# Experts of a decoder layer: down products one block behind, in three single-pass products, with low parts cut on POOL

## The chip, the cores and the metric

One core of a Trainium2 chip. The metric is the device time of one launch in microseconds; smaller is better. All arithmetic is on float32 data.

## The reference

One decoder layer over 1024 prompt tokens and 8 sample tokens, width 1024. A combined projection feeds twelve dilated and eight stick-breaking attention heads and two gates; the heads' outputs are merged and added to `x`. Then comes a mixture of experts, an input embedding and a last norm. The part that matters here:

```python
def expert_block(args):
    xi, ei = args
    return (jax.nn.silu(xi @ w_gate[ei]) * (xi @ w_up[ei])) @ w_down[ei]

def channel_and_ple(x, p, ...):
    x = x + hier_moe(rmsnorm(x, g_moe), ...)
    gate = jax.nn.sigmoid(rmsnorm(x, g_ple) @ w_pg)
    return x + gate * (p @ w_pp)
```

Each token goes to the top two experts of its group. There are 32 experts, with `w_gate` and `w_up` of 1024 x 512 and `w_down` of 512 x 1024. Tokens are sorted by expert and handled in blocks of 128 rows, each with the weights of one expert.

## The kernel before

The kernel is written engine by engine, with semaphores set by hand. Its stages follow each other: `norm_in`, `project`, `stick_and_gates`, `dilated`, `decode`, `merge`, `residual`, `route`, `experts`, `finish`. In the trace a tile of the experts has the prefix `x_`, one of the last stage `f_`, one of the residual stage `r_`.

`residual` (L1433) makes `h`, nine tiles of 128 rows (the last has 8), which stays in SBUF until `finish` adds the experts' rows to it. `route` (L1550) writes the normed rows to DRAM in expert order (`xs`), and a table with each block's expert and first row.

`experts` (L1742) runs 32 blocks here. For one block SP loads the rows `x` (512 KB), `wg` and `wu` each in two halves of 1024 KB, and `wd` (2048 KB). TensorE multiplies float32 in two ways. A plain product of 128x512 takes float32 operands as they are (down, L1854). The other way (`products`, L82) splits each operand in a high part, rounded to the type fp32r, and the rest, and adds three single-pass products:

```python
    pe.matmul(out, w_low, m_high, start=first, stop=False)
    pe.matmul(out, w_high, m_low, start=False, stop=False)
    return pe.matmul(out, w_high, m_high, start=False, stop=last)
```

ACT makes the high parts (`high`, L1885: `wgh`, `wuh`; `xh`, L1901), and DVE the low parts by a subtraction (`low`, L1932: `wgl`, `wul`; `xl`, L1926). Gate and up have 8 k-slices each, so 24 products each; down has 4 k-slices and two halves of the output, 8 plain products in the code, each of which stands as two records in the trace.

The order of work is fixed for each engine in a function `step`. PE runs gate and up of a block (`gate_up`), turns the next block's rows (`turn`, L1829), then turns the hidden rows `hm` of the first block (`tph`, L1847) and multiplies them (`down`). DVE's `hidden` (L1942) makes `hm`, its `hidden_T` (L1947) copies the turned rows to `hT`. ACT takes the sigmoid (L1878) and copies the output out of PSUM (`output`, L1891), and POOL stores it to `ys` (L1981) at a row that it loads from the table. `passes` does the first two steps outside the loop and two steps for each turn of it. `need(eng, sem, v)` is a wait that is left out where `v` is not positive.

`finish` (L1991) gathers each token's two rows from `ys`, adds them to `h` (L2173), loads and splits the weights of the last projections in five pieces of 1 MB, and waits on DVE for the last gains `gf` before the second tile is turned.

Of the kernel before, what the change touches and what calls it, by code (L numbers as in the profile page):

```python
# [1432 lines left out]
def residual(nc, g, x_of):  # L1433

    ctx = ExitStack()
    with ctx:
# [113 lines left out]
def route(nc, g):  # L1550
# [5 lines left out]
    with ctx:  # L1556
# [95 lines left out]
        def _(dve):  # L1652
# [85 lines left out]
            then(dve.tensor_scalar(metaf[:, 2:3], metaf[:, 2:3], -1.0, None, ALU.add))  # L1738
# [3 lines left out]
def experts(nc, g):  # L1742
# [6 lines left out]
    with ctx:  # L1749
# [5 lines left out]
        wd = sb("wd", [P, 2, KF, D])  # L1755
        gm = sb("gm", [P, KD])
# [4 lines left out]
        hT = sb("hT", [P, KF, P])  # L1761
# [17 lines left out]
        Wd = g["w_down"].rearrange("a e (k p) f -> (a e) p k f", p=P)
        block = ctx.enter_context(nc.Block())  # L1780

        def pairs(eng):

            return eng.value_load(meta_row[0:1, 2:3], min_val=(-(-ASG // P) + 1) // 2 - 1,
                                  max_val=(MAXBLK + 1) // 2 - 1) + 1

        def passes(eng, step, end):


            n = pairs(eng)  # L1790
            for j in range(2):
                step(0, j)
            with eng.Fori(1, n) as it:
                for j in range(2):
                    step(it, j)
            if end:
                end(n)

        @block.sync
        def _(sp):  # L1800
            with nc.allow_non_contiguous_dma(reason="1024 gains, once"):
                sp.dma_start(gm[:, :], g["g_moe"].rearrange("a (k p) -> p (a k)", p=P)).then_inc(gm_in, 16)

            def step(it, b):
# [11 lines left out]
                need(sp, y_full, it * 4 + (2 * b - 2))  # L1816
# [5 lines left out]
        def _(pe):  # L1822
            def turn(it, b):

                pe.wait_ge(x_in[b], it * 16 + 16)
                for c in range(2):
                    need(pe, xT_full, it * 4 + (2 * b + c - 1))
                    for k in range(4):
                        last = pe.transpose(tpx[c][:, k, :], x[:, b, (c * 4 + k) * P:(c * 4 + k + 1) * P], ident[:, :])  # L1829
                    last.then_inc(tpx_full, 1)  # L1830

            def gate_up(n):

                pe.wait_ge(xl_full, n + 1)
                need(pe, hm_full, n)
                for bank, wh, wl, cut, s in ((G, wgh, wgl, gl_full, g_full), (U_, wuh, wul, ul_full, u_full)):
                    pe.wait_ge(cut, n * 2 + 2)
                    for k in range(KD):
                        last = products(pe, bank[:, :], xh[:, k, :], xl[:, k, :], wh[:, k, :], wl[:, k, :],
                                        k == 0, k == KD - 1)  # L1840
                    last.then_inc(s, 1)

            def down(p_, b, n):
                pe.wait_ge(hm_full, n + 1)
                need(pe, hT_full, n)
# [505 lines left out]
```

## Time and profile before

| | |
|---|---|
| median of 3 runs | 2381.64 us (2381.1 to 2393.33) |
| the profiled execution | 2380.5 us |
| its span | 2378.9 us |
| PE busy | 2012.9 us, 85% |
| DVE busy | 1098.7 us, 46% |
| ACT busy | 850.9 us, 36% |
| POOL busy | 277.5 us, 12% |
| mean granted TensorE clock | 0.92 |

The span is from the first instruction to the last of the profiled execution, and 1.6 us of its time lie around it. Busy shares are means over stages with different limits. A matmul record is longer than the distance to the next one, since they are pipelined, so a cost of PE is read from start to start.

### The profile page before, as it was taken

The page shows a single profiled execution, that of the slowest core. Times are in us where ns is not written, and L with a number is a line of the kernel's source. Part 1 is how long each engine was busy: PE and PEld are TensorE (multiplying, and loading weights), DVE is VectorE, ACT ScalarE, POOL GpSimd, SP SyncE. Part 2 cuts the span into 40 slices and gives each one's busy share as a digit, 9 for nine tenths or more (in the row PEclk, how much of TensorE's full clock was granted, in tenths as well). Part 3 has the DMA queues.
Part 4 walks back from the last instruction along what each step waited for, and adds up shares of the span by engine and source line. Part 5 has one row for each costly group of instructions (what it writes and reads, how often), then busy time and mean ns, then how long its engine had stood idle before and what let it go on. Part 6 is the DMA issues. An engine that isn't in the chain of part 4 may idle for free. (4 is left out here: it accounts for less than half of the span.)

```text
span 2378.9 us, 27707 instructions
## 1 busy us (share of the span) xinstructions
PE 2012.9 (85%) x10172; PEld 1572.0 (66%) x10172; DVE 1098.7 (46%) x1363; ACT 850.9 (36%) x1171; POOL 277.5 (12%) x356
## 2 busy tenths in 40 slices
PE   6999999698989879993288994499999999998598
PEld 5999999687878857772177452366666666665485
DVE  5212121255546545552342214466666666664564
ACT  4111111255546415450031100344444444452354
POOL 0110111143334310001012002100000000000210
PEclk8999999899999959896588996699999999999699
DMA  3343443434111042206334102999999999994530
GB/s 116 113 136 106 124 123 108 144 107 145 37 63 37 28 89 41 41 1 162 102 106 163 53 19 73 341 374 360 348 347 350 352 353 357 351 349 156 194 99 37
DMA packets 222238, 392.70 MB, mean 165 GB/s; under 512 B 29468, under 2 KB 100620, under 8 KB 222165
## 3 DMA queue, kind: packets, MB, share of 16 engines
q1 hardware_dynamic: 202916, 325.28, 40.3%
q0 software_dynamic: 14928, 50.60, 6.7%
q10 hardware_dynamic: 4320, 15.85, 1.7%
q8 instruction: 46, 0.75, 0.1%
q14 instruction: 28, 0.22, 0.0%
HBM read 321.02 MB, written 78.35 MB: 168 GB/s over the span
## 5 line engine op out<-in xcount | busy, mean ns | idle before, releaser
L1854 PE MATMUL x_Y<-x_wd,x_hT 128*128 128x512 f32 x512 | 229.8, 602 | 34.4 <-DVE x_hT L1947 34.4
L86 PE MATMUL p_acc<-uh,p_wl 128*128 128x344 f32 x720 | 234.9, 326 | 13.2 <-DVE ul L292 9.1
L88 PE MATMUL p_acc<-uh,p_wh 128*128 128x344 f32 x720 | 230.6, 320 | 0.0
L87 PE MATMUL p_acc<-ul,p_wh 128*128 128x344 f32 x720 | 230.4, 320 | 0.0
L1854 PEld LDWEIGHTS x_Y<-x_wd,x_hT 128*128 128x128 f32 x512 | 95.2, 191 | 150.1 <-issue 150.1
L304 DVE COPY p_zk<-p_tp 128x512 f32<-128x512 f32 (+1 forms) x90 | 44.2, 547 | 304.5 <-PE p_tp L225 304.5
L1932 DVE TENSOR_TENSOR x_wgl<-x_wg,x_wgh 128x2048 fp32r<-128x2048 f32 x64 | 146.3, 2286 | 69.9 <-ACT x_wgh L1885 69.9
L268 ACT ACTIVATE p_zc<-p_acc 128x344 f32<-128x344 f32 x90 | 41.2, 458 | 321.8 <-PE p_acc L88 321.8
L561 PE MATMUL g_acc<-uh,g_wl 128*128 128x344 f32 x384 | 131.2, 342 | 21.6 <-ACT u L594 19.5
L86 PEld LDWEIGHTS p_acc<-uh,p_wl 128*128 128x128 f32 x720 | 135.8, 189 | 18.1 <-issue 14.8
L1932 DVE TENSOR_TENSOR x_wul<-x_wu,x_wuh 128x2048 fp32r<-128x2048 f32 x64 | 143.5, 2282 | 0.0
L1485 PE MATMUL r_acc<-r_w,mT 128*128 128x512 f32 (+1 forms) x288 | 128.5, 606 | 10.0 <-DMA r_w<-in_w_out 10.0
L1885 ACT ACTIVATE x_wgh<-x_wg 128x2048 fp32r<-128x2048 f32 x64 | 118.9, 1906 | 49.1 <-DMA x_wg<-in_w_gate 49.1
L88 PEld LDWEIGHTS p_acc<-uh,p_wh 128*128 128x128 f32 x720 | 135.9, 189 | 0.0
L87 PEld LDWEIGHTS p_acc<-ul,p_wh 128*128 128x128 f32 x720 | 135.9, 189 | 0.0
L561 PE MATMUL g_acc<-ul,g_wh 128*128 128x344 f32 x384 | 129.7, 338 | 0.0
L561 PE MATMUL g_acc<-uh,g_wh 128*128 128x344 f32 x384 | 129.5, 337 | 0.0
L86 PE MATMUL x_G<-x_wgh,x_xl 128*128 128x512 f32 x256 | 114.8, 448 | 9.9 <-DVE x_xl L1926 9.9
L1885 ACT ACTIVATE x_wuh<-x_wu 128x2048 fp32r<-128x2048 f32 x64 | 118.4, 1896 | 0.1
L655 POOL TENSOR_TENSOR s_z<-s_z,s_w 128x1024 f32<-128x1024 f32 (+7 forms) x64 | 91.8, 1434 | 208.9 <-DVE s_w L682 208.9
L682 DVE TENSOR_TENSOR_SCAN s_w<-s_w,s_r 128x1024 f32<-128x1024 f32 (+7 forms) x64 | 86.8, 1356 | 54.9 <-ACT s_w L631 54.4
L820 PE MATMUL d_S<-d_k,d_q 64*128 64x256 f32 (+3 forms) x272 | 94.8, 499 | 17.4 <-DMA d_v<-ztok 16.9
(320 smaller groups left out, 4089.2 us busy)
## 6 DMA issues: line engine op xcount, KB each, us to landing
x_wg<-in_w_gate SPq DMA_DIRECT2D x64, 1024.0 KB, 7.3
x_wu<-in_w_up SPq DMA_DIRECT2D x64, 1024.0 KB, 7.3
x_wd<-in_w_down SPq DMA_DIRECT2D x32, 2048.0 KB, 12.1
x_x<-xs SPq DMA_DIRECT2D x32, 512.0 KB, 9.8
ys<-x_y POOLq DMA_DIRECT2D x32, 512.0 KB, 5.5
zT<-p_zc ACTq DMA_DIRECT2D x30, 516.0 KB, 3.4
p_w<-in_w_in SPq DMA_DIRECT2D x30, 512.0 KB, 5.5
ztok<-p_zk POOLq DMA_DIRECT2D x30, 512.0 KB, 4.6
```

Of the source, the lines that this page charges most:

```text
L86: pe.matmul(out, w_low, m_high, start=first, stop=False)
L87: pe.matmul(out, w_high, m_low, start=False, stop=False)
L88: return pe.matmul(out, w_high, m_high, start=False, stop=last)
L304: dve.tensor_copy(zk[0:r, b, t0:t0 + m, :], tp[j % 2][0:r, 0:m, :]).then_inc(zk_full, 1)
L561: last = pe.matmul(acc[grp % 2][:, 0:NS], lhs[:, c % 2, kk, :], rhs[:, kk, t], start=(x == 0), stop=(x == M - 1), skip_group_check=True)
L655: pool.tensor_tensor(z[:, u % ZB, 0:n], z[:, u % ZB, 0:n], w[:, u % WB, 0:n], ALU.subtract).then_inc(al_full, 1)
L682: dve.tensor_tensor_scan(w[:, u % WB, 0:n][:, ::-1], w[:, u % WB, 0:n][:, ::-1], r[:, u % 2, 0:n][:, ::-1], 0.0, ALU.add, ALU.add).then_in ...
L820: last = pe.matmul(S[x // 2][:, c:c + n], q[:, b, x, i * P:(i + 1) * P], k[:, b, x, key:key + n], start=True, stop=True, skip_group_check= ...
L1485: last = pe.matmul(acc[t % 2][0:r, c * 512:(c + 1) * 512], mT[:, k, t * P:t * P + r], w[:, k, c * 512:(c + 1) * 512], start=(k == 0), stop ...
L1854: last = pe.matmul(Y[c][:, :], hT[:, k, :], wd[:, b, k, c * 512:(c + 1) * 512], start=(k == 0), stop=(k == KF - 1))
L1885: act.activation(wh[:, HALVES[half], :], w[:, HALVES[half], :], ACT.Copy).then_inc(full, 1)
L1932: dve.tensor_tensor(wl[:, s, :], w[:, s, :], wh[:, s, :], ALU.subtract).then_inc(full, 1)
```

## The change

The down products are made in the same three-product way. For this `wd` is split too: ACT makes `wdh`, one k-slice at a time, and POOL makes `wdl` by a subtraction; the hidden rows are split to `hh` on ACT and `hl` on DVE. PE's step now has gate of block n, turning the hidden rows of block n-1, up of block n, turning the rows of block n+1, and down of block n-1. ACT copies the output of yet a block earlier at the start of its step, and issues the store to `ys` itself, with the row that it loads. DVE makes both halves of `wgl` ahead of `hm` and `xT`. Both halves of `wg` and `wu` are waited for one by one on PE.

The weights of the experts are read with rows p*k+j to partition p instead of j*128+p, so a partition reads four or eight rows that lie together, and PE turns columns with a stride to match.

To make room in SBUF, `h` isn't kept there over the experts: `residual` stores its nine tiles to `h_kept` in DRAM and `finish` loads them again, two ahead of the weight pieces and seven behind them, before `gf`. Four steps instead of two stand outside the loop.

```diff
+                if t >= 2:
+                    sp.dma_start(g["h_kept"][(t - 2) * P:(t - 1) * P, :], h[:, t - 2, :]).then_inc(h_out, 16)
+            for t in range(TT - 2, TT):
+                sp.wait_ge(h_full, t + 1)
+                sp.dma_start(g["h_kept"][t * P:t * P + rows(t), :], h[0:rows(t), t, :]).then_inc(h_out, 16)
+            sp.wait_ge(h_out, 16 * TT)
...
+        Wg = g["w_gate"].rearrange("a e (p k) f -> (a e) p k f", p=P)
+        Wu = g["w_up"].rearrange("a e (p k) f -> (a e) p k f", p=P)
+        Wd = g["w_down"].rearrange("a e (p k) f -> (a e) p k f", p=P)
...
+            n = eng.value_load(meta_row[0:1, 2:3], min_val=0, max_val=(MAXBLK + 1) // 2 - MINPAIR) + MINPAIR
+            for it in range(PEEL):
+                for j in range(2):
+                    step(it, j)
+            with eng.Fori(PEEL, n) as it:
                 for j in range(2):
                     step(it, j)
...
-                need(sp, y_full, it * 4 + (2 * b - 2))
+                need(sp, dl_full, it * 8 + (4 * b - 4))
                 sp.dma_start(wd[:, b, :, :], w(Wd)).then_inc(d_in[b], 16)
...
+                by_k = x[:, b, :].rearrange("t (p k) -> t k p", k=KD)
...
+            def gate(n):
                 pe.wait_ge(xl_full, n + 1)
+                need(pe, gs_full, n)
+                gate_or_up(n, G, wgh, wgl, gl_full, g_full)
...
+            def turn_hidden(n):
                 pe.wait_ge(hm_full, n + 1)
-                need(pe, hT_full, n)
+                need(pe, hl_full, n)
+                by_k = hm[:, :].rearrange("t (p k) -> t k p", k=KF)
                 for k in range(KF):
-                    last = pe.transpose(tph[:, k, :], hm[:, k * P:(k + 1) * P], ident[:, :])
+                    last = pe.transpose(tph[:, k, :], by_k[:, k, :], ident[:, :])
                 last.then_inc(tph_full, 1)
...
+            def down(n):
+                pe.wait_ge(hl_full, n + 1)
+                need(pe, y_read, n * 2)
+                for k in range(KF):
+                    pe.wait_ge(dl_full, n * 4 + (k + 1))
+                    for c in range(2):
+                        cols = slice(c * 512, (c + 1) * 512)
+                        last = products(pe, Y[c][:, :], hh[:, k, :], hl[:, k, :], wdh[:, k, cols], wdl[:, k, cols],
+                                        k == 0, k == KF - 1)
+                    last.then_inc(d_used, 1)
...
+                one, two = lag(it, j, 1), lag(it, j, 2)
+                if one:
+                    gate(one[0])
+                if two:
+                    turn_hidden(two[0])
+                if one:
+                    up(one[0])
+                turn(it * 2 + j, j, it)
+                if two:
+                    down(two[0])
...
+            def high_down(n, b, it):
+                act.wait_ge(d_in[b], it * 16 + 16)
+                for k in range(KF):
+                    need(act, d_used, it * 8 + (4 * b + k - 3))
+                    act.activation(wdh[:, k, :], wd[:, b, k, :], ACT.Copy).then_inc(dh_full, 1)
+
+            def high_hidden(n):
+                act.wait_ge(tph_full, n + 1)
+                need(act, d_used, n * 4)
+                act.activation(hh[:, :, :], tph[:, :, :], ACT.Copy).then_inc(hh_full, 1)
...
+            def output(n, b, it):
+                act.wait_ge(d_used, n * 4 + 4)
                 for c in range(2):
-                    act.wait_ge(y_full, n * 2 + c + 1)
                     act.activation(y[:, b, c * 512:(c + 1) * 512], Y[c][:, :], ACT.Copy).then_inc(y_read, 1)
+                need(act, y_out[1 - b], it * 16 + 16 * b)
+                act.wait_ge(y_read, n * 2 + 2)
+                row = act.value_load(meta_row[0:1, bass.ds(n * 4 + 1, 1)], min_val=0, max_val=ASG)
+                act.dma_start(ys[bass.ds(row, P), :], y[:, b, :]).then_inc(y_out[b], 16)
...
+                if three:
+                    output(*three)
+                if two:
+                    high_down(*two)
+                if one:
+                    sigmoid(one[0])
+                if two:
+                    high_hidden(two[0])
                 high(new, wg, wgh, wg_in, g_full, gh_full)
                 act.wait_ge(xT_full, new * 2 + 2)
+                need(act, u_full, new)
                 act.activation(xh[:, :, :], xT[:, :, :], ACT.Copy).then_inc(xh_full, 1)
                 high(new, wu, wuh, wu_in, u_full, uh_full)
...
+            def low_hidden(n):
+                dve.wait_ge(hh_full, n + 1)
+                dve.tensor_tensor(hl[:, :, :], tph[:, :, :], hh[:, :, :], ALU.subtract).then_inc(hl_full, 1)
...
+                if one:
+                    gated(one[0])
+                if two:
+                    low_hidden(two[0])
+                for half in range(2):
+                    low(new, half, wg, wgh, wgl, gh_full, gl_full)
+                if one:
+                    hidden(one[0])
                 turn(new)
-                low(new, 1, wg, wgh, wgl, gh_full, gl_full)
                 low_x(new)
                 for half in range(2):
                     low(new, half, wu, wuh, wul, uh_full, ul_full)
...
+            def low_down(n, b):
+                for k in range(KF):
+                    pool.wait_ge(dh_full, n * 4 + (k + 1))
+                    pool.tensor_tensor(wdl[:, k, :], wd[:, b, k, :], wdh[:, k, :], ALU.subtract).then_inc(dl_full, 1)
+
+            def step(it, j):
+                two = lag(it, j, 2)
+                if two:
+                    low_down(two[0], two[1])
...
+            def load_h(t):
+                sp.dma_start(h[0:rows(t), t, :], g["h_kept"][t * P:t * P + rows(t), :]).then_inc(hs_in[t], 16)
+
             for t in range(2):
                 sp.dma_start(pt[0:rows(t), t % 2, :], p_of(t)).then_inc(p_in[t % 2], 16)
+                load_h(t)
             for n, (raw, w, _, _) in enumerate(pieces):
                 need(sp, wl_full, n - 2)
                 sp.dma_start(raw, w).then_inc(piece_in[n], 16)
+            for t in range(2, TT):
+                load_h(t)
...
+                dve.wait_ge(hs_in[t], 16)
...
-            g["h"] = ctx.enter_context(nc.sbuf_tensor("h", [P, TT, D], F32, side="right"))
```

ACT, the second step in the loop of `experts`. Before:

```order
L1878 ACTIVATE x_sg<-x_G 128x512
L1884 ISA
L1885 ACTIVATE x_wgh<-x_wg 128x2048 x2
L1900 ISA
L1901 ACTIVATE x_xh<-x_xT 128x1024
L1885 ACTIVATE x_wuh<-x_wu 128x2048 x2
L1888 ISA
L1890 REGISTER_ALU
L1891 ACTIVATE x_y<-x_Y 128x512 x2
```

The same step of the changed kernel, from the output's copies on:

```order
L1934 ACTIVATE x_y<-x_Y 128x512 x2
L1936 ISA
L1937 ISA
L1937 TENSOR_LOAD meta_row
L1937 ISA x2
L1938 ISA
L1938 DMA ys<-x_y 128x1024
L60 REGISTER_ALU
L1924 ACTIVATE x_wdh<-x_wd 128x1024
```

Three more `x_wdh` follow, then `x_sg`, the new `x_hh`, and `x_wgh`, `x_xh` and `x_wuh` as before. The output's copies moved from the end of the step to its beginning, with the table's load and the store's issue behind them.

DVE, the same step. Before:

```order
L1936 TENSOR_TENSOR x_gs<-x_sg,x_G 128x512
L1930 ISA
L1932 TENSOR_TENSOR x_wgl<-x_wg,x_wgh 128x2048
L1942 TENSOR_TENSOR x_hm<-x_gs,x_U 128x512
L1947 COPY x_hT<-x_tph 128x512
L1920 TENSOR_TENSOR x_xT<-x_tpx,x_gm 128x512
L1919 REGISTER_ALU
L1920 TENSOR_TENSOR x_xT<-x_tpx,x_gm 128x512
L1932 TENSOR_TENSOR x_wgl<-x_wg,x_wgh 128x2048
```

And of the changed kernel:

```order
L1995 TENSOR_TENSOR x_gs<-x_sg,x_G 128x512
L2005 TENSOR_TENSOR x_hl<-x_tph,x_hh 128x512
L1988 ISA
L1990 TENSOR_TENSOR x_wgl<-x_wg,x_wgh 128x2048
L1988 REGISTER_ALU
L1990 TENSOR_TENSOR x_wgl<-x_wg,x_wgh 128x2048
L2001 TENSOR_TENSOR x_hm<-x_gs,x_U 128x512
L1978 TENSOR_TENSOR x_xT<-x_tpx,x_gm 128x512 x2
```

The second `x_wgl` moved ahead of `x_hm` and both `x_xT`; `x_xl` and two `x_wul` follow in both.

## Rows read from the trace of the kernel before

**Rows 1.** Page, 40 slices of 59.5 us: busy tenths of PE and of DMA.

```profile
PE   6999999698989879993288994499999999998598
...
DMA  3343443434111042206334102999999999994530
```

**Rows 2.** Stretches: bounds, length, busy us per engine, clock, DMA share, GB/s.

```profile
1600.00:1700.00 100.00, 94.91 (x358) 63.54 (x359) 63.84 (x49) 48.44 (x40) 2.66 (x5) 1.00 0.94 347
...
1805.00:1810.00 5.00, 3.83 (x21) 2.79 (x21) 3.15 (x5) 0.57 (x1) 0.00 (x0) 1.00 1.02 414
```

**Rows 3.** Waits, 1700 to 1909 us: total us, times, longest.

```profile
PE x_Y L1854 <- DVE x_hT L1947: 10.7, 10, 1.2
```

**Rows 4.** Tile x_G: ns min/median/max, first and last start.

```profile
L1878 ACT ACTIVATE x_sg<-x_G x32: 597/597/598, 1529.9 to 2177.2; 128x512 f32<-128x512 f32 x32
```

**Rows 5.** Timeline of one block: start, us, engine, line, operation, names.

```profile
1801.09 0.40 PE L86 MATMUL x_U<-x_wuh,x_xl 128*128 128x512 f32 x1
...
1806.45 0.40 PE L88 MATMUL x_U<-x_wuh,x_xh 128*128 128x512 f32 x1
...
1806.69 1.04 PE L1829 MATMUL x_tpx<-ident,x_x 128*128 128x128 f32 x8
...
1807.72 0.66 PE L1847 MATMUL x_tph<-ident,x_hm 128*128 128x128 f32 x4
...
1809.55 7.13 PE L1854 MATMUL x_Y<-x_wd,x_hT 128*128 128x512 f32 x16 [1.17 <-DVE x_hT L1947]
...
1816.11 0.80 PE L86 MATMUL x_G<-x_wgh,x_xl 128*128 128x512 f32 x1
```

**Rows 6.** Groups, 1700 to 1909 us: count | busy us, mean ns | idle.

```profile
L1932 DVE TENSOR_TENSOR x_wgl<-x_wg,x_wgh 128x2048 fp32r<-128x2048 f32 x21 | 48.0, 2287 | 12.2 <-ACT x_wgh L1885 12.2
...
L1885 ACT ACTIVATE x_wuh<-x_wu 128x2048 fp32r<-128x2048 f32 x20 | 36.9, 1895 | 0.0
...
L1920 DVE TENSOR_TENSOR x_xT<-x_tpx,x_gm 128x512 f32<-128x512 f32 x20 | 12.8, 680 | 0.0
...
L1901 ACT ACTIVATE x_xh<-x_xT 128x1024 fp32r<-128x1024 f32 x10 | 10.6, 1058 | 48.6 <-DVE x_xT L1920 48.6
...
L1942 DVE TENSOR_TENSOR x_hm<-x_gs,x_U 128x512 f32<-128x512 f32 x10 | 6.9, 686 | 8.8 <-PE x_U L88 8.8
```

**Rows 7.** Source line 1784, the counter's load: ns min/median/max, starts.

```profile
L1784 ACTq TENSOR_LOAD <-meta_row x1: 475/475/475, 1503.7 to 1503.7; - x1
...
L1784 ACTq FUSED_REGOPS  x1: 175/175/175, 1504.2 to 1504.2; - x1
```

**Rows 8.** Source line 1807, an address loaded on SP's queue.

```profile
L1807 SPq TENSOR_LOAD <-meta_row x32: 273/1424/1822, 1504.9 to 2132.4; - x32
```

**Rows 9.** Timeline of ACT at 301 us: a DMA issued from its queue.

```profile
301.10 0.34 ACTq L274 DMA_DIRECT2D zT<-p_zc  x1
```

**Rows 10.** POOL's groups over the whole span, columns as before.

```profile
L655 POOL TENSOR_TENSOR s_z<-s_z,s_w 128x1024 f32<-128x1024 f32 x8 | 19.0, 2376 | 38.2 <-DVE s_w L682 38.2
```

**Rows 11.** Source line 662, a 128x1024 difference on DVE.

```profile
L662 DVE TENSOR_TENSOR g_wl<-g_w,g_wh x16: 1211/1276/3052, 453.8 to 798.7; 128x1024 fp32r<-128x1024 f32 x16
```

**Rows 12.** Timeline, 557 to 560 us: POOL and DVE together.

```profile
557.69 2.37 POOL L655 TENSOR_TENSOR s_z<-s_z,s_w 128x1024 f32<-128x1024 f32 x1 [4.17 <-DVE s_w L682]
...
558.11 3.03 DVE L662 TENSOR_TENSOR g_wl<-g_w,g_wh 128x1024 fp32r<-128x1024 f32 x1
...
560.02 1.43 POOL L650 TENSOR_TENSOR s_z<-s_z,s_causal 128x128 f32<-128x128 f32 x1
```

**Rows 13.** Chain of waits, last stage: start, us, what.

```profile
2236.17 0.43 PE f_gate L88
```

**Rows 14.** DMA issues: names, queue, count, KB each, median us to landing.

```profile
f_gf<-in_g_final SPq DMA_DIRECT2D x1, 512.0 KB, 9.0
```

**Rows 15.** Timeline of the last stage.

```profile
2230.84 0.47 SPq L2050 DMA_DIRECT2D f_gf<-in_g_final  x1
...
2242.70 1.22 DVE L2194 TENSOR_TENSOR f_uT<-f_tp,f_gp 128x1024 f32<-128x1024 f32 x1
```

More of the change, by code:

```diff
@@ L1780, in experts @@
         block = ctx.enter_context(nc.Block())
-        def pairs(eng):
-            return eng.value_load(meta_row[0:1, 2:3], min_val=(-(-ASG // P) + 1) // 2 - 1,
-                                  max_val=(MAXBLK + 1) // 2 - 1) + 1
+        PEEL = 2
         def passes(eng, step, end):
[L1790 to L1793, printed above, removed]
+            n = eng.value_load(meta_row[0:1, 2:3], min_val=0, max_val=(MAXBLK + 1) // 2 - MINPAIR) + MINPAIR
[3 more added lines that the diff above has]
+            with eng.Fori(PEEL, n) as it:
@@ L1797, in passes, with lag @@
                 end(n)
+        def lag(it, j, back):
+            new = it * 2 + j
+            if isinstance(it, int) and new < back:
+                return None
+            return new - back, (j - back) % 2, it + (j - back) // 2
         @block.sync
@@ L1835, in gate_up, with up @@
+            def up(n):
                 need(pe, hm_full, n)
[L1836 to L1843, printed above, removed]
+                gate_or_up(n, U_, wuh, wul, ul_full, u_full)
@@ L1850, in down @@
-                pe.wait_ge(hT_full, n + 1)
-                for c in range(2):
-                    need(pe, y_read, n * 2 - 1 + c)
-                    for k in range(KF):
-                        last = pe.matmul(Y[c][:, :], hT[:, k, :], wd[:, b, k, c * 512:(c + 1) * 512],
-                                         start=(k == 0), stop=(k == KF - 1))
-                    last.then_inc(y_full, 1)
-            def step(it, j):
-                behind = j or not isinstance(it, int)
-                p_, b, n = (it, 0, it * 2) if j else (it - 1, 1, it * 2 - 1)
-                if behind:
-                    gate_up(n)
-                turn(it, j)
-                if behind:
-                    down(p_, b, n)
@@ new lines, in step @@
+            def step(it, j):
+                one, two = lag(it, j, 1), lag(it, j, 2)
[8 more added lines that the diff above has]
+                    down(two[0])
+            def end(np_):
+                last = np_ * 2 - 1
+                gate(last)
+                turn_hidden(last - 1)
+                up(last)
+                down(last - 1)
+                turn_hidden(last)
+                down(last)
@@ L1893, in step @@
             def step(it, j):
-                behind = j or not isinstance(it, int)
-                p_, b, n = (it, 0, it * 2) if j else (it - 1, 1, it * 2 - 1)
+                one, two, three = lag(it, j, 1), lag(it, j, 2), lag(it, j, 3)
                 new = it * 2 + j
-                if behind:
-                    sigmoid(n)
+                if three:
[4 more added lines that the diff above has]
+                    sigmoid(one[0])
@@ L1910, in _ @@
+                output(last - 2, 1, np_ - 2)
+                high_down(last - 1, 0, np_ - 1)
+                sigmoid(last)
+                high_hidden(last - 1)
+                output(last - 1, 0, np_ - 1)
+                high_down(last, 1, np_ - 1)
+                high_hidden(last)
+                output(last, 1, np_ - 1)
             passes(act, step, end)
@@ L2000, in finish @@
         C = D // 2
+        h = sb("h", [P, TT, D])
+        hs_in = [sem(f"h_in{t}") for t in range(TT)]
         wpgh, wpgl = (sb(n, [P, KD, D], F32R) for n in ("wpgh", "wpgl"))
```

95 lines of the change are left out of this document (40 added, 55 removed).

## The prediction

> **What bounds the kernel now.** I read the page's slices first: from about 1506 to 2196 us one stage, the experts, holds PE and the DMA engines at nine tenths or more together [rows 1]. It is the only long stage that the change rewrites. The reader is to see that shares do not tell which of the two ends last, so the waits come next: in ten blocks PE waits 10.7 us for x_hT, 1.07 each, and neither PE nor ACT or DVE waits for a transfer [rows 3]. The DMA engines move 347 GB/s over a hundred us and 414 in a stretch where they have work queued [rows 2], so they have room. One block moves 7.34 MB (four halves of 1024 KB, x_wd of 2048, x_x and ys of 512 each): at 400 GB/s 18.4 us.
>
> The length of a block is read from the sigmoid x_sg: 32 of them start between 1529.9 and 2177.2 us [rows 4], so 647.3 / 31 = 20.9 us. The timeline of one block fills that with PE alone [rows 5]: the 24 products of up begin from 1801.09 to 1806.45, 0.233 apart (5.36 / 23), gate costs as much, so 48 x 0.233 = 11.2; transposes 1.04 and 0.66; the wait for x_hT 1.17; the down products, eight of two records each, 6.56 (1809.55 to 1816.11), 0.82 a product; the first gate product 0.80 for 0.40, which delays those behind it by some 0.3. Sum 20.9. **PE sets the block.**
>
> **PE after the change.** Eight products at 0.82 become 24 single-pass ones, whose spacing stands above: 5.6 for 6.56. The wait of 1.17 goes, since x_hm is a step old when PE turns it and up stands between its halves and their use. PE needs 72 x 0.233 + 1.7 = 18.5 us, 2.4 less. The transposes now read with a stride; no row shows that. Between nothing and double (1.7 more) PE is still under the loop below, so I price it at nothing: what hides it is PE's own slack of 5 us, without which it costs up to 1.7 a block.
>
> **ACT and DVE after the change.** What is late next is a loop that exists now but has slack. In one step ACT does, in order: x_y twice, an address load with its DMA, x_wdh four times, x_sg, x_hh, x_wgh twice, x_xh, x_wuh twice. DVE does x_gs, x_hl, x_wgl twice, x_hm, x_xT twice, x_xl, x_wul twice. x_xh waits for x_xT, which stands on DVE behind both x_wgl; the next step's x_y stands on ACT behind x_wuh. The terms:
>
> - x_y: 2 x 0.6 = 1.2, by x_sg, which is of its shape [rows 4].
> - Load and issue, new on ACT's queue and behind a wait for its own x_y: load 0.48, register work 0.18 [rows 7], issue 0.34 [rows 9], together 1.0. The load's upper bound is 1.42, SP's median just behind its DMA issues [rows 8]; ACT's issue is a step old, so I take 0.48. Queued behind it are all of ACT's copies. The removed POOL issue gave PE nothing: POOL waited for ACT.
> - x_wdh: same shape as x_xh, 1.06 each, so 4.2; x_sg and x_hh 0.6 each [rows 4].
> - x_wgh, x_wuh 1.9 each [rows 6], x_wgl 2.29, x_hm 0.69, x_xT 0.68, x_xh 1.06.
>
> With nothing in the way: 1.2 + 1.0 + 4.2 + 1.2 + 1.9 (the first x_wgh), then DVE 4.6 + 0.7 + 1.4, then ACT 1.1 + 3.8 = 21.1; back-to-back instructions overlap by up to 0.1, hand-overs cost up to 0.1, and I take 20.7. PE's gain of 2.4 is already gone here: this loop is within 0.2 of the old block.
>
> **The shared port.** The new x_wdl is 128x1024 with two inputs in SBUF on POOL. Its nearest row is L655's form of the same shape, 2.38 us [rows 10], 9.5 for four. Does that run beside DVE's x_wgl, which also reads two SBUF tiles? The trace has such pairs. g_wl on DVE takes 1.21 at the least and up to 3.05 [rows 11]. At 558.11 it started 0.42 after POOL's s_z, which held on to 560.06: 1.95 of waiting, and 3.03 - 1.95 = 1.08 of work. POOL's next s_z of 128x128, begun at 560.02, took 1.43 instead of under half a microsecond: it waited for DVE in turn [rows 12]. The engines alternate; they do not share. By the Trainium skill's page "SBUF — State Buffer", section "Who interferes with whom", the second read interface is an exclusive lock held for a whole instruction; the trace agrees.
>
> So in a block, POOL's four x_wdl start when the first x_wdh is done, 1.2 + 1.0 + 1.1 = 3.3 us into ACT's step, and alone would end at 12.8. DVE asks for x_wgl at 9.5. It waits for the third x_wdl, runs one x_wgl, waits for the fourth, runs the other: 3.3 us lost. The loop reads 3.3 + 9.5 (POOL) + 4.6 (both x_wgl) + 0.7 + 1.4 + 1.1 + 3.8 = 24.4, less the same 0.4: **24.0 us a block**, 3.1 more than now. x_wul and x_xl fall outside that stretch. The DMA engines (7.34 MB in 24.0) and PE (18.5) both get slack.
>
> The Trainium skill's page "GPSIMD Engine Reference", section 3.1, measures a two-input operation on GpSimd at about 2.6 cycles an element. At the 1.2 GHz it gives, that is an estimate of 2.2 us for 1024; by it the block would be 23.4 and the kernel 19 us less. The row of 2.38 is this kernel's own, and the sum goes by it.
>
> **Two ends.** Steps 0 and 1 have none of ACT's and POOL's new work, 2 x 3.1 saved; the last block's x_wdl (9.5) has nothing over it. About +4, bounds -6 and +12.
>
> **h through DRAM.** Nine stores of 512 KB in the residual stage go on SP's queue, each behind a load; that stage leaves the DMA engines nearly idle [rows 1] and its last store is one tile of 8 rows: nothing, bounded by one landing of some 3 us. In the last stage two h loads go ahead of the weights and seven, 3.2 MB, ahead of f_gf. f_gf took 9.0 us to land [rows 14]; at 400 GB/s the loads put 8 us on it. DVE waits for it before f_uT at 2242.70, where f_gf, issued at 2230.84, had been there for 3 us [rows 15]. So +5, and 2 for the first two loads: +7, bounds 0 and 13. The larger runs of the expert weights (four and eight rows together) are at nothing: nobody waits for them, before or after.
>
> **Sum**, against the profiled execution's own 2380.5 us (the median of the three runs is 1.1 above it): 31 x 3.1 = 96, + 4, + 7 = +107: **2488 us**. Above and below 0.5%, 12 us, a measurement can tell it from no change.
>
> **Rivals.**
> 1. DVE goes first whenever the port comes free. Then it waits once, 1.0, and not twice: block 21.7, 31 x 0.8 + 11 = +36, 2417. For: a single kind of hand-over is on record. Against: POOL's s_z at 560.02 had come second and ran next.
> 2. POOL and DVE don't disturb each other in this stage, or the four x_wdl are over before DVE asks: block 20.7 or 20.5, 31 x -0.4 + 11: 2380, no change. Against it stand [rows 11, 12] and x_wdl's 9.5 us against the 6.2 between first x_wdh and x_wgl; it decides where x_wdl takes under 1.6 us.
> 3. Not slower at all: the loop has a slack that I don't see (ACT's copies run ahead), and PE's 18.5 holds: 31 x -2.4 + 11 = -63, 2317. It needs x_xh to come 2.2 us sooner. Against: every copy's order is fixed.
> 4. PE falls to its lower clock. Idle for 5 us in each block, it could come back at 1.2 GHz, where the last stage's products of this shape stand 0.43 apart [rows 13]. If gate and up both run so: 48 x 0.43 + 24 x 0.233 + 1.7 = 27.9, 31 x 7.0 + 11 = +228, 2609. If gate alone does, PE ends its block inside the 24.0 and it costs nothing. The Trainium skill's page "TensorE: Matmul & The Clock Gate", rules for authors, warns of such gaps between bursts. I find it less likely for both, because PE would then be busy all the time.
>
> The upper bound of the load adds 0.9 a block (28 us); an x_wdl slower by a tenth (its output type has no row on POOL) 29: 2545 together.
>
> **How the numbers follow.** The forecast 0.70, rival 1 0.12, rival 2 0.07, rival 3 0.05, rival 4 0.06. The range holds the forecast with its bounds and rival 1, 2400 to 2545, and leaves the other three out, 0.18. Faster 0.05, no change 0.07, slower 0.88.
>
> **What would show it.** Right: x_sg 24 us apart; x_wgl well over its 2.29 in the mean, near 4; some x_wdl over 4 us; PE's longest wait for x_xl, not for x_hl; the DMA share down to eight tenths; POOL at 300 us more or above; f_uT's second start later by 5. Wrong: x_wgl at 2.29 (rival 2), x_wdl long and x_wgl short (1), gate and up at 0.43 (4), ACT idle before x_y. If x_sg stands 24 apart with x_wgl undisturbed, the load on ACT was the cost and my reason fails.

## The result, and the profile after

| | before | after |
|---|---|---|
| median of four runs each, us | 2385.8 (2381.1 to 2393.33) | 2481.29 (2479.04 to 2487.31) |
| ratio | | 1.040, 95% interval 1.036 to 1.044 |
| profiled execution, us | 2380.5 | 2481.67 |
| block of the experts, mean of 31 (us) | 20.9 | 23.4 |

The changed kernel is slower by 4.0%. The forecast was 2488, in the range 2400 to 2545; the profiled execution came out 6 us under it.

The two kernels were timed beside each other. Beside the experiments below the kernel before has medians of 2389.3, 2393.0 and 2389.4 us, and all ratios are to it.

The slices of the page first, as in [rows 1] but of 62.0 us each, and one window of the experts with the columns of [rows 2]:

```profile
PE   5999999698898699953689953888888888887498
...
DMA  3434433541210403034343119787777877873720
```

```profile
1700.00:1940.00 240.00, 202.97 (x864) 162.29 (x863) 172.84 (x102) 142.37 (x131) 119.73 (x42) 0.93 0.77 308
```

In the experts (the long run of eights in PE) DMA is at seven and eight tenths where [rows 1] have nines, and PE at eight: the transfers wait for something else, and so does PE. The granted clock is 0.93 of full, for 1.00 before. The sigmoid, as in [rows 4] (nanoseconds min/median/max, first and last start):

```profile
L1911 ACT ACTIVATE x_sg<-x_G x32: 572/577/599, 1536.3 to 2262.6; 128x512 f32<-128x512 f32 x32
```

(2262.6 - 1536.3) / 31 = 23.43 us a block, for 20.88. 31 x 2.55 = 79 of the 101 us that the profiled executions lie apart. The mean of 31 hides one thing: the first two distances are 19.55 and 22.60, since the first two steps lack part of the new work, and the other 29 have a mean of 23.59. Where blocks are compared below it is by the mean of 31; where the forecast of one block is judged, by 23.59.

Now one block, in the timeline (start, length, what; in brackets the idle time before and what ended it), from one x_xh to the next:

```profile
1803.57 1.06 ACT L1954 ACTIVATE x_xh<-x_xT 128x1024 fp32r<-128x1024 f32 x1 [7.67 <-DVE x_xT L1978]
1804.53 3.70 ACT L1918 ACTIVATE x_wuh<-x_wu 128x2048 fp32r<-128x2048 f32 x2
...
1808.13 1.06 ACT L1934 ACTIVATE x_y<-x_Y 128x512 f32<-128x512 f32 x2
...
1809.97 0.34 ACTq L1938 DMA_DIRECT2D ys<-x_y  x1
...
1810.44 3.90 ACT L1924 ACTIVATE x_wdh<-x_wd 128x1024 fp32r<-128x1024 f32 x4 [1.24 <-issue]
...
1811.57 11.57 POOL L2037 TENSOR_TENSOR x_wdl<-x_wd,x_wdh 128x1024 fp32r<-128x1024 f32 x4 [11.98 <-ACT x_wdh L1924]
...
1814.86 0.69 DVE L1995 TENSOR_TENSOR x_gs<-x_sg,x_G 128x512 f32<-128x512 f32 x1 [3.90 <-ACT x_sg L1911]
...
1817.14 8.15 DVE L1990 TENSOR_TENSOR x_wgl<-x_wg,x_wgh 128x2048 fp32r<-128x2048 f32 x2 [1.00 <-ACT x_wgh L1918]
...
1825.22 0.68 DVE L2001 TENSOR_TENSOR x_hm<-x_gs,x_U 128x512 f32<-128x512 f32 x1
...
1825.82 1.28 DVE L1978 TENSOR_TENSOR x_xT<-x_tpx,x_gm 128x512 f32<-128x512 f32 x2
...
1827.13 1.06 ACT L1954 ACTIVATE x_xh<-x_xT 128x1024 fp32r<-128x1024 f32 x1 [8.21 <-DVE x_xT L1978]
```

This is the loop, 23.56 us round, and each step of it is read off from start to start: x_xh 0.96, both x_wuh 3.60, both x_y with the load and the issue 2.31, the first x_wdh 1.13, then 5.57 to the start of x_wgl and 8.08 to its end, x_hm 0.60, x_xT and the hand-over 1.31. The two rows of 11.57 (POOL's x_wdl) and 8.15 (DVE's x_wgl) are the ones to look at. Two such subtractions take 4.49 where POOL is idle (the x_wul below), and here 8.15. Where each one waited is told by their tiles (rows of x_wgl and x_wul on DVE, of x_wdl on POOL):

```profile
L1990 DVE TENSOR_TENSOR x_wgl<-x_wg,x_wgh x64: 2286/3744/4494, 1519.9 to 2245.3; 128x2048 fp32r<-128x2048 f32 x64
```
```profile
L1990 DVE TENSOR_TENSOR x_wul<-x_wu,x_wuh x64: 2283/2289/2294, 1529.2 to 2256.7; 128x2048 fp32r<-128x2048 f32 x64
```
```profile
L2037 POOL TENSOR_TENSOR x_wdl<-x_wd,x_wdh x128: 2352/2415/4485, 1550.8 to 2284.6; 128x1024 fp32r<-128x1024 f32 x128
```

x_wul is the same operation on the same shape, in a stretch where POOL is idle, and never takes over 2.3. x_wgl, beside POOL's x_wdl, takes 3.74 in the median and up to 4.49; one x_wdl of a block takes 4.49 too, for 2.4: about its own time behind one x_wgl's. The row of x_gs in the timeline shows what is not shared: it lies inside the stretch of x_wdl and keeps its 0.69 (so do all 32 of them), with one input in SBUF and the other (x_G) in PSUM.

The waits between 1700 and 1940 us, ten blocks (total us, times, longest):

```profile
PE x_G L87 <- DVE x_xl L1984: 36.7, 10, 4.8
ACT x_wdh L1924 <- issue: 12.8, 10, 1.3
```

PE waits for x_xl, 4.8 at the longest, never for x_hl, and once, for 0.2, for x_wdl. ACT waits 1.27 a block in which the profile names nobody: its own row load and DMA issue. In the last stage the gains f_gf now take 13.7 us to land, and DVE waits 4.99 for them (views as in [rows 14, 15]):

```profile
f_gf<-in_g_final SPq DMA_DIRECT2D x1, 512.0 KB, 13.7
```

```profile
2341.65 1.23 DVE L2266 TENSOR_TENSOR f_uT<-f_tp,f_gp 128x1024 f32<-128x1024 f32 x1 [4.99 <-DMA f_gf<-in_g_final]
```

### The profile page after: what moved, and what is told of

The parts are those of the page before. It is cut to its first block and busy times, and to the rows that moved or that the text cites. A ratio compares the mean times of both kernels' runs of the same rounds, so it can differ in the third digit from the quotient of the medians.

```text
span 2480.0 us, 28841 instructions
## 1 busy us (share of the span) xinstructions
PE 2020.7 (81%) x10428; PEld 1656.9 (67%) x10428; DVE 1206.8 (49%) x1363; ACT 984.8 (40%) x1332; POOL 627.8 (25%) x451
## 5 line engine op out<-in xcount | busy, mean ns | idle before, releaser
L2037 POOL TENSOR_TENSOR x_wdl<-x_wd,x_wdh 128x1024 fp32r<-128x1024 f32 x128 | 367.0, 2903 | 415.8 <-ACT x_wdh L1924 415.8
L1990 DVE TENSOR_TENSOR x_wgl<-x_wg,x_wgh 128x2048 fp32r<-128x2048 f32 x64 | 250.9, 3958 | 64.3 <-ACT x_wgh L1918 64.3
L87 PE MATMUL p_acc<-uh,p_wl 128*128 128x344 f32 x720 | 234.5, 326 | 14.1 <-DVE ul L293 9.8
L87 PE MATMUL x_G<-x_wgh,x_xl 128*128 128x512 f32 x256 | 124.2, 485 | 126.4 <-DVE x_xl L1984 126.4
L87 PEld LDWEIGHTS x_G<-x_wgh,x_xl 128*128 128x128 f32 x256 | 59.6, 233 | 153.9 <-issue 121.2
L1924 ACT ACTIVATE x_wdh<-x_wd 128x1024 fp32r<-128x1024 f32 x128 | 124.9, 1047 | 39.9 <-issue 39.9
L1954 ACT ACTIVATE x_xh<-x_xT 128x1024 fp32r<-128x1024 f32 x32 | 33.8, 1056 | 251.9 <-DVE x_xT L1978 251.9
L316 POOL DMA_DIRECT2D ztok<-p_zk x30 | 28.0, 933 | 394.4 <-DVE p_zk L305 380.1
```

What stands on the lines that cost most here:

```text
L1924: act.activation(wdh[:, k, :], wd[:, b, k, :], ACT.Copy).then_inc(dh_full, 1)
L1990: dve.tensor_tensor(wl[:, s, :], w[:, s, :], wh[:, s, :], ALU.subtract).then_inc(full, 1)
L2037: pool.tensor_tensor(wdl[:, k, :], wd[:, b, k, :], wdh[:, k, :], ALU.subtract).then_inc(dl_full, 1)
```

## The experiments

In this section GpSimd is the engine that the traces call POOL, VectorE is DVE, ScalarE ACT, TensorE PE and SyncE SP. Theory: POOL's x_wdl and DVE's x_wgl exclude each other at their reads of SBUF, and this lies in the loop above, with ACT's load and issue as a second term. Rivals: that ACT's and POOL's mere lengths close the loop; that the move, without any split, is what costs; that the larger runs of the layout matter. Twelve runs follow, one of them the changed kernel once more. All have the changed kernel's order and h in DRAM where nothing else is said.

**GpSimd only writes.** x_wdl becomes two memsets with two tiny subtractions (a wait between the two pairs is not shown):

```
-pool.tensor_tensor(wdl[:, k, :], wd[:, b, k, :], wdh[:, k, :], ALU.subtract)
+pool.tensor_tensor(wdl[:, k, 0:4], wd[:, b, k, 0:4], wdh[:, k, 0:4], ALU.subtract)
+pool.memset(wdl[:, k, 8:D].bitcast(F32), 0.0)       # then the same on 4:8 and 8:D
```

> The changed kernel, but GpSimd only writes: instead of each subtraction of x_wdl it does two memsets of 128x1016 and two subtractions of 128x4, about 2.2 to 2.5 us a slice, so nearly as long as the subtraction (2.38). The low part of the down weights is left out. Theory (the two subtractions, GpSimd's and VectorE's, wait for each other at their reads of SBUF): x_wgl goes from a mean of 3.96 us back to 2.29, x_wdl's place takes no longer than its own time, and the block goes from 23.4 to about 20.7 us, the kernel from 2481 to about 2400. Rival (the loop is closed by ScalarE's row load and DMA issue and by GpSimd's mere length): x_wgl may fall, but the block stays at 23.0 to 23.4 and the kernel at 2470 to 2481.

Measured: 2378.93 us in one run, block 20.26.

```profile
L1912 ACT ACTIVATE x_sg<-x_G x32: 570/574/602, 1536.5 to 2164.5; 128x512 f32<-128x512 f32 x32
```

```profile
1823.59 0.20 POOL L2041 TENSOR_TENSOR x_wdl<-x_wd,x_wdh 128x4 fp32r<-128x4 f32 x1
...
1824.63 1.35 POOL L2038 TENSOR_TENSOR x_wdl<-x_wd,x_wdh 128x4 fp32r<-128x4 f32 x1
...
1825.92 0.94 POOL L2039 MEMSET x_wdl<- 128x1016 f32 x1
...
1826.10 2.29 DVE L1991 TENSOR_TENSOR x_wgl<-x_wg,x_wgh 128x2048 fp32r<-128x2048 f32 x1 [0.17 <-ACT x_wgh L1919]
...
1826.95 1.50 POOL L2041 TENSOR_TENSOR x_wdl<-x_wd,x_wdh 128x4 fp32r<-128x4 f32 x1
```

The timeline is the experiment in small. The memset at 1825.92 keeps its 0.94 beside x_wgl, and x_wgl keeps 2.3 beside memsets (2.33 at the most in all 64). The subtraction of 128x4 at 1824.63, of 0.20 elsewhere, takes 1.35, until x_wgl ends at 1825.92; the one at 1826.95 takes 1.50, until the second x_wgl ends at 1828.39. GpSimd's queue is as long as before (2.2 us a slice for 2.4), so its length isn't what cost: the reads are. 3.2 us a block come back, and the block is 0.4 shorter than the 20.7 expected.

**GpSimd copies, one input.** In two forms: one copy a slice, then, since the first said nothing, two.

```
-pool.tensor_tensor(wdl[:, k, :], wd[:, b, k, :], wdh[:, k, :], ALU.subtract)
+pool.tensor_copy(wdl[:, k, 8:D], wdh[:, k, 8:D])    # once, behind a subtraction of 128x8; or twice, each behind one of 128x4
```

> The changed kernel, with a copy of x_wdh (one input) on GpSimd in place of each two-input subtraction of x_wdl, behind a subtraction of 128x8 (the low part of the down weights is left out). With GpSimd writing only, VectorE kept its x_wgl at 2.29 us. Theory (what is shared is the second read): with one input GpSimd does not hold it; x_wgl 2.3 us, block 20.2, kernel about 2380. Rival (any read by GpSimd holds it): x_wgl at 3 to 3.5, since the copy is shorter (1.1 to 1.3 us), block 21 to 22, kernel 2400 to 2430.

Measured: 2371.09 us in one run, block 19.95; x_wgl 2.29. But the timeline shows that the last copy was over before x_wgl began, so neither side was put to the test:

```profile
1817.49 1.03 POOL L2038 CAST x_wdl<-x_wdh 128x1016 fp32r<-128x1016 f32 x1
...
1819.49 4.49 DVE L1990 TENSOR_TENSOR x_wgl<-x_wg,x_wgh 128x2048 fp32r<-128x2048 f32 x2 [1.00 <-ACT x_wgh L1918]
```

> As the run in which GpSimd only wrote, with each memset replaced by a copy (one input) of x_wdh, about 1.03 us each, so that a slice takes 2.3 to 2.4 us and the copies stand beside VectorE's x_wgl (the low part of the down weights is left out). Theory (only an instruction with two inputs takes the second read): copies keep 1.03 us and x_wgl 2.29 beside each other; the tiny two-input subtractions of 128x4 wait for x_wgl to end; block about 20.2, kernel about 2378. Rival (any read of GpSimd excludes VectorE): x_wgl above 3 us or copies above 2 us, block 21.5 or more, kernel above 2400.

Measured: 2433.66 us in one run, block 21.64.

```profile
L1912 ACT ACTIVATE x_sg<-x_G x32: 572/577/599, 1546.1 to 2217.0; 128x512 f32<-128x512 f32 x32
```

```profile
1807.39 4.73 DVE L1991 TENSOR_TENSOR x_wgl<-x_wg,x_wgh 128x2048 fp32r<-128x2048 f32 x2 [1.00 <-ACT x_wgh L1919]
...
1807.86 2.12 POOL L2041 TENSOR_TENSOR x_wdl<-x_wd,x_wdh 128x4 fp32r<-128x4 f32 x1
...
1809.92 3.09 POOL L2042 CAST x_wdl<-x_wdh 128x1016 fp32r<-128x1016 f32 x1
```

My theory of the "second read" falls and the rival holds: the copy at 1809.92, one input, takes 3.09 for 1.03, since it stands until the second x_wgl is done. VectorE waits too: x_wgl takes 2.58 in the mean of the window and up to 3.13, for 2.31 and 2.33 beside memsets. So GpSimd's one-input copy and VectorE's two-input subtraction exclude each other too; a memset and VectorE don't. Not all of the time is lost at the port. The block is 1.4 us longer than with memsets, and only about 0.5 of it lies in the two x_wgl. About 0.9 lies in ACT's waits for the transfer of x_wg, 16.9 us in eleven blocks for 7.9 in twelve: SP issues x_wd's load only when GpSimd's last copy is done, and x_wg's stands behind it in the queue. The Trainium skill's page "SBUF — State Buffer", section "Who interferes with whom", has it so: VectorE's instruction with two SBUF inputs contends with a GpSimd instruction that reads SBUF, not with one that only writes. Both of these runs agree, with 3.09 and 0.94 us. For the kernel it changes nothing, since its x_wdl has two inputs.

**x_wdl on VectorE.**

```
-pool: low_down(two[0], two[1])
+dve:  low_down(two[0], two[1])      # ahead of gated(one[0]); in the end ahead of gated and of the last low_hidden
```

> The changed kernel, with the subtractions of x_wdl on VectorE (4 of 128x1024, about 1.2 us each, ahead of x_gs) and none on GpSimd. Theory (shared reads): x_wgl at 2.29, no instruction above its own time; VectorE has 4.9 us more work but gets back 3.4 of x_wgl and had idle time before x_gs and x_hl; block 20.7, kernel about 2400 (2385 to 2425). Rival (the work itself is too much for the loop, wherever it stands): block 23 to 24.5, kernel 2470 to 2515.

Measured: 2383.93 us (2373.79 to 2394.58, ten runs), 0.995 of the kernel before (0.992 to 0.998); block 20.05, for 20.7 expected. The second row is the window 1700 to 1940 us, its columns those of [rows 2].

```profile
L1911 ACT ACTIVATE x_sg<-x_G x32: 571/576/600, 1555.6 to 2177.2; 128x512 f32<-128x512 f32 x32
```

```profile
1700.00:1940.00 240.00, 220.17 (x1003) 177.10 (x1002) 212.17 (x169) 168.50 (x156) 0.00 (x0) 1.00 0.96 366
```

The same arithmetic, and 3.4 us a block are back: 4.9 us of added work on the busier engine cost about 0.1 (20.05, beside 19.95 in the run with one copy a slice), where 9.6 us on the idle one cost 3.4 (23.43 - 20.05). The window's clock is 1.00 again.

**Store of ys from GpSimd.**

```
-act: row = act.value_load(...); act.dma_start(ys[...], y[:, b, :])
+pool: row = pool.value_load(...); pool.wait_ge(y_read, ...); pool.dma_start(ys[...], y[:, b, :])   # ahead of low_down
```

> The changed kernel, with the row load and the issue of the store of ys moved from ScalarE back to GpSimd, ahead of its x_wdl. Theory (ScalarE's 1.27 us between x_y and x_wdh are a term of the loop): x_wdh starts 1.27 earlier in each block and the block goes to about 22.2, the kernel to about 2443 (2435 to 2455). Rival (only the shared port and GpSimd set the block, and GpSimd now takes the load itself): no change, 2475 to 2485.

Measured: 2459.79 us (2455.69 to 2476.84), 1.030 (1.023 to 1.037); block 22.65, 0.78 less and not 1.2, and the kernel above the range expected.

```profile
L1912 ACT ACTIVATE x_sg<-x_G x32: 584/598/599, 1534.4 to 2236.6; 128x512 f32<-128x512 f32 x32
```

```profile
1799.23 3.90 ACT L1925 ACTIVATE x_wdh<-x_wd 128x1024 fp32r<-128x1024 f32 x4
...
1800.57 11.95 POOL L2041 TENSOR_TENSOR x_wdl<-x_wd,x_wdh 128x1024 fp32r<-128x1024 f32 x4
...
1805.93 8.74 DVE L1988 TENSOR_TENSOR x_wgl<-x_wg,x_wgh 128x2048 fp32r<-128x2048 f32 x2 [1.00 <-ACT x_wgh L1919]
```

ACT's 1.27 us are gone, but from the start of x_wdh to the end of the second x_wgl it is now 15.44 us, for 14.85 in the block of the changed kernel shown above. The pair of x_wgl itself is not a steady sign: it takes 6.7 to 8.7 from block to block, as x_wgl starts sooner or later, and the stretch takes 15.4 in those blocks too. The 0.59 lie on POOL, whose x_wdl let x_wgl through last: it begins 0.21 later against x_wdh, and its first x_wdl, right behind the issue of the store, takes 2.79 for 2.41. 1.27 - 0.59 = 0.68 of the measured 0.78. So half of ACT's gain was lost because the load and the issue now stand ahead of x_wdl on POOL, which is the rival in part.

**The move alone.** x_hh in f32, eight products as before, no x_wdh, x_wdl, x_hl:

```
-last = products(pe, Y[c][:, :], hh[:, k, :], hl[:, k, :], wdh[:, k, cols], wdl[:, k, cols], ...)
+last = pe.matmul(Y[c][:, :], hh[:, k, :], wd[:, b, k, cols], ...)
-need(sp, dl_full, it * 8 + (4 * b - 4))
+need(sp, d_used, it * 8 + (4 * b - 4))
```

> The move alone: the down products stand behind the next block's gate and up as in the changed kernel, h goes through DRAM, but the down weights and the hidden values stay f32 and whole, 8 products instead of 24, no x_wdh, x_wdl, x_hl. Theory (TensorE bound the kernel of before, and 1 to 1.5 us of it a block was a wait for the turned hidden values that the move covers): block 19.5, kernel about 2360 (2345 to 2385). Rival (the wait only moves elsewhere, to the low parts of x): block 20.9, kernel 2395 to 2410, above the kernel before by the h loads.

Measured: 2462.57 us (2461.55 to 2472.09), 1.030 (1.024 to 1.036); block 22.76. Neither theory nor rival. SyncE's queue (SPq) and ACT's wait:

```profile
L1910 ACT ACTIVATE x_sg<-x_G x32: 597/598/599, 1540.5 to 2246.2; 128x512 f32<-128x512 f32 x32
```

```profile
1710.55 0.33 SPq L1831 DMA_DIRECT2D x_wd<-in_w_down  x1
1712.39 0.33 SPq L1825 DMA_DIRECT2D x_x<-xs  x1
1712.98 0.91 SPq L1829 DMA_DIRECT2D x_wg<-in_w_gate  x2
```

```profile
ACT x_wgh L1917 <- DMA x_wg<-in_w_gate: 34.1, 10, 6.4
```

x_wd's buffer is used by products that now stand two steps behind, so its load waits until 1710.55, and x_x, x_wg and x_wu of the next block stand behind it in the queue. ACT then waits for x_wg's transfer, up to 6.4 us. The mean of 22.76 is made of two kinds of block: they alternate between 19.3 and 25.7 to 27.5 us, and why only every other one pays is not shown. The next run moves that one load:

```
 for dst, src, cut, done in ((wg, ...), (wu, ...)): ...
-need(sp, d_used, it * 8 + (4 * b - 4)); sp.dma_start(wd[:, b, :, :], w(Wd))
+if one: load_down(*one)             # the x_wd of the block before, its own row of the table
```

> The move alone (f32 down products behind the next block's gate and up), but the load of a block's x_wd is issued one step later, behind the next block's x_wg and x_wu. In the run before, SyncE's queue waited at x_wd for the down products two blocks back, until 1710.55, and the x_x, x_wg and x_wu behind it landed late (ScalarE's x_wgh waited for their transfers 34.1 us in ten blocks). Theory (the place of that wait in the queue made the move alone slow, not the products): block 19.5 to 20.2, kernel 2360 to 2385. Rival (TensorE's f32 down products between up and the next gate hold back x_xT and the low parts whatever the loads do): block stays at 22 to 22.8, kernel 2440 to 2465.

Measured: 2355.83 us (2351.44 to 2368.01), 0.986 (0.981 to 0.990); block 19.43.

```profile
L1920 ACT ACTIVATE x_sg<-x_G x32: 597/598/600, 1535.1 to 2137.3; 128x512 f32<-128x512 f32 x32
```

```profile
1705.10 2.53 SPq L1829 DMA_DIRECT2D x_wu<-in_w_up  x2
1709.45 0.33 SPq L1837 DMA_DIRECT2D x_wd<-in_w_down  x1
1711.29 0.33 SPq L1825 DMA_DIRECT2D x_x<-xs  x1
```

```profile
1700.00:1940.00 240.00, 240.00 (x935) 165.24 (x934) 157.78 (x111) 129.83 (x113) 0.00 (x0) 1.00 0.96 377
```

3.3 us a block from the place of one load. PE is busy for the whole 240 us of the window, and the block is what the prediction's terms give for it: 11.2 + 1.7 + 6.56 = 19.5. So the move by itself is a gain of 1.5 us a block, the wait of [rows 3] and some start-up, once nothing queues behind it.

**The old layout,** on the version with x_wdl on VectorE:

```
-"a e (p k) f -> (a e) p k f"
+"a e (k p) f -> (a e) p k f"        # and so for g_moe, x and hm
```

> The kernel with x_wdl on VectorE, with the old layout of the expert weights, x and h (row k*128+p on partition p, as before the change). With the new layout this stage moves 366 GB/s at a DMA share of 0.96 between 1700 and 1940 us, 381 per full share; the kernel before moves 352 at 0.95, 370. Theory (that kernel is now bound by the DMA engines and the new layout is worth 3% of their rate): block 20.6 against 20.05, kernel 15 to 20 us slower than it. Rival (the share is high but something else ends last; forecast: the layout costs and gains nothing): the same within 5 us.

Measured: 2375.53 us (2371.91 to 2383.03), 0.993 (0.990 to 0.996); block 20.04.

```profile
L1911 ACT ACTIVATE x_sg<-x_G x32: 572/577/601, 1537.4 to 2158.5; 128x512 f32<-128x512 f32 x32
```

```profile
1700.00:1940.00 240.00, 225.61 (x1006) 179.94 (x1005) 212.17 (x168) 168.54 (x156) 0.00 (x0) 0.97 1.01 366
```

The block is the same within 0.01. The layout is worth nothing here, neither for the transfers nor for the transposes that read with a stride: PE isn't the bound here, so the block alone can't tell their cost, but one transpose of x takes 0.274 us in the median of the changed kernel and took 0.272 before. DMA at 1.01 of its share for the same 366 GB/s says that it would have been worth something had the transfers been the bound: an argument, not shown.

**f_gf first,** beside the changed kernel once more:

```
+sp.dma_start(gf[:, :], g["g_final"]...)
 for t in range(2, TT): load_h(t)
-sp.dma_start(gf[:, :], g["g_final"]...)
```

> The changed kernel, with the load of f_gf ahead of the loads of h in the last stage. Theory (VectorE's first product with f_gf waits for that load, 4.99 us in the profile of the changed kernel): that wait is gone or under 1, the kernel 5 to 6 us faster than the changed kernel run beside it. Rival (the loads of h then come as late for x_mix): 0 to 1 us.

> The changed kernel once more, beside the others: 2481 us, block 23.43.

Measured: 2484.56 us (2468.09 to 2492.28), 1.038 (1.032 to 1.044), beside 2484.15 (2475.39 to 2501.11), 1.041 (1.035 to 1.046). By the times, nothing. The profiles say more: f_gf's landing, then x_sg and the last products f_yo, of this run and of the changed kernel beside it:

```profile
f_gf<-in_g_final SPq DMA_DIRECT2D x1, 512.0 KB, 9.1
```

```profile
L1911 ACT ACTIVATE x_sg<-x_G x32: 571/577/598, 1540.5 to 2266.9; 128x512 f32<-128x512 f32 x32
```

```profile
L2299 DVE SCALAR_TENSOR_TENSOR f_yo<-f_h,f_st,f_gf x9: 1273/1285/1286, 2361.5 to 2473.8; 128x1024 f32<-128x1024 f32 x8, 8x1024 f32<-8x1024 f32 x1
```

```profile
L1911 ACT ACTIVATE x_sg<-x_G x32: 572/577/599, 1531.1 to 2257.3; 128x512 f32<-128x512 f32 x32
```

```profile
L2299 DVE SCALAR_TENSOR_TENSOR f_yo<-f_h,f_st,f_gf x9: 1273/1285/1286, 2356.1 to 2470.3; 128x1024 f32<-128x1024 f32 x8, 8x1024 f32<-8x1024 f32 x1
```

From the last x_sg to the last f_yo it is 2473.8 - 2266.9 = 206.9, and 2470.3 - 2257.3 = 213.0 without the edit: 6.1 us less, about the 5 to 6 expected, and VectorE no longer waits for f_gf. But this run came to its first x_sg at 1540.5 and the other at 1531.1, with the same code up to there. Six us in one stage lie below what these medians can tell.

**Two versions meant to beat both.** x_wdl on VectorE, store from GpSimd, f_gf first:

> A version meant to beat both: the changed kernel with x_wdl on VectorE, the store of ys with its row load on GpSimd, and f_gf's load ahead of those of h in the last stage. Theory: 5 to 6 us from f_gf, and ScalarE's 1.27 us a block out of a loop that the DMA engines (share 0.96) now share the bound with, so only 0.2 to 0.4 of it a block: about 2368 (2360 to 2378), under the kernel before by about 1%. Rival (the transfers alone bound the block): only the gain of f_gf, 2378 (2374 to 2382).

Measured: 2350.78 us (2345.44 to 2360.39), 0.983 (0.979 to 0.987); block 19.34.

```profile
L1912 ACT ACTIVATE x_sg<-x_G x32: 585/592/600, 1534.5 to 2134.0; 128x512 f32<-128x512 f32 x32
```

```profile
1700.00:1940.00 240.00, 227.65 (x1039) 183.15 (x1038) 219.01 (x173) 175.68 (x164) 6.92 (x13) 1.00 0.97 379
```

Better than expected: with x_wdl off the port, ACT's 1.27 brought 0.71 a block. So the block of 20.05 was still the loop's and not the transfers', although DMA stood at 0.96 there and moved 366 GB/s; it stands at 0.97 now and moves 379. A share near one was no bound here.

> The move alone with the late load of x_wd (f32 down products, nothing split), and f_gf's load ahead of those of h. Theory: block 19.43 as in the move alone, 5 to 6 us less in the last stage: about 2350 (2344 to 2356), level with the version with x_wdl on VectorE (2350.8), with a third of the code and no split of the down weights. Rival (f_gf's load costs as much elsewhere): 2356.

Measured: 2355.93 us (2340.73 to 2366.14), 0.984 (0.980 to 0.989); block 19.39. Level with the one above within the measurement, and with the move alone without the edit of f_gf (2355.83), whose 5 us can't be seen in the medians; in the profiles they can, from the last x_sg to the last f_yo 203.9 us for 209.0.

## Why the prediction was right

**The mechanism** stands as told: the loop over ACT, DVE and POOL, with DVE held twice a block. Every sign that the prediction named for it is there. It was shown three times over: by x_wgl beside x_wul, by GpSimd's writes in place of its reads, and by the same subtractions on VectorE. Rivals 2 and 3 and the reading that lengths alone close the loop are out. Rival 1 (DVE first at each hand-over) is out by the median of x_wgl.

**The block** was to be 24.0 and is 23.59 once the first two are past. The terms before overlap add up to 24.4, and the loop shown takes 23.56, step by step: to the first x_wdh 3.44 for 3.3 (load and issue took 1.27 and not 1.0, part of it hidden), x_wdl and x_wgl 13.65 for 9.5 + 4.6 = 14.1, x_hm and x_xT 1.91 for 2.1, x_xh and x_wuh 4.56 for 4.9. So the overlap of back-to-back instructions takes 0.8 off the terms, where 0.4 was priced. 31 x 0.4 = 12 us too much in the sum. By the Trainium skill's page "GPSIMD Engine Reference", section 3.1, the estimate had been 23.4. It comes as near for a reason that doesn't hold: an undisturbed x_wdl takes 2.35 to 2.42 us, the row's figure and not 2.2. A subtraction of 128x4 takes 0.20, and with that added to 2.2 the page's rate gives 2.4 too, an estimate.

**Without the port** I took 20.7; the runs show 20.26, 20.05 and 19.95. The same fault, overlap priced too low, with the same sign.

**PE** at 18.5 and out of the bound: yes. Behind the wait for x_xl it came back at its lower clock for part of gate (in the block above gate's products stand 0.43 us apart from 1806.60 to 1808.73 and 0.23 from 1809.10 on; over the window it is 0.93 of full): the mild form of rival 4, absorbed as said. Runs whose block is 20.3 or less show a clock of 1.00 in the same window, but for 0.97 with the old layout.

**The ends** were +4. From the first x_x issue to the first f_y issue the profile has 87.7 more. The prediction took 31 full blocks and counted the short first steps among the ends; by that count 31 x (23.59 - 20.88) = 84 are the blocks and 3.7 the ends. **The finish** was +7 and is 7.7 in the profile, of which VectorE's wait for f_gf is 4.99. **The residual stage** was at nothing, and is: from its first product r_acc to the first x_x issue it is 206.9 us, for 207.2 before.

**What was left over**, 5.7 us, was there before the residual stage began (6.0 at its first product), where the change touches nothing. The changed kernel run again began the experts at 1506.4 (first x_x issue) for 1511.8, the kernel before at 1506.1. That is scatter, and luck: the total came out 6 us off with one term 12 us too high, because an unrelated 6 us made up for half of it.

**What I had not seen** is the queue. In the move alone the wait of x_wd's load, taken over from the old order, cost 3.3 us a block. In the changed kernel that wait ends with x_wdl, and ACT never waits for a transfer between 1700 and 1940 us, so the prediction was not hurt. With memsets or two copies, where GpSimd is busy for as long in a shorter block, it shows: ACT waits 0.7 and 1.5 us a block for x_wg. The prediction spoke only of ACT's queue.

## What to carry to other kernels

Before giving work to an idle GpSimd, look at what VectorE does in that stretch: if it reads two SBUF tiles there, GpSimd's reads of SBUF don't run beside it but in turn with it, and 4.9 us on VectorE can be cheaper than 9.6 on GpSimd. Split a change with three parts into its parts: here the move, once its load was moved too, gained 1.5 us a block, the split of the products gained nothing over it (20.05 for 19.43), and its place on GpSimd lost 3.4. The split without the move was not tried. When a consumer moves back by a step, move the load that waits for its buffer as well, or everything behind that load in the queue moves too.

## What the runs showed of the hardware

- GpSimd's one-input copy from SBUF waits for VectorE's two-input subtraction as a two-input one does (3.09 us for 1.03); its memset doesn't (0.94 beside x_wgl). A two-input subtraction of only 128x4 is held as well (1.35 and 1.50 us for 0.20).
- VectorE's operations with one input in SBUF and one in PSUM run beside GpSimd's two-input ones undisturbed (x_gs 0.69 in all 32 blocks).
- An x_wdl right behind a DMA issue on GpSimd took 2.79 us for 2.41.
- TensorE's granted clock, mean from 1700 to 1940 us: 0.93 in the changed kernel, where gate's first products stand 0.43 us apart (1.2 GHz) behind waits of up to 4.8; 1.00 with x_wdl on VectorE (waits of up to 1.7 us); 0.97 in that kernel with the old layout (up to 1.8).
- DMA engines at a share of 0.96 moved 366 GB/s, and at 0.97 379 in another version of the same stage.
- Stages with the same code end 25 us apart in different executions (first x_x issue at 1506.4 in the changed kernel run again, at 1531.1 with x_wdl on VectorE).
